# A hybrid decoder layer: level 3's differences between two halves of the masked copies, and a GpSimd product in two halves

## The reference

```
def gla_chunked(q, k, v, log_a):
    def step(state, inp):
        qc, kc, vc, ac = inp
        bc = jnp.cumsum(ac, axis=1)
        diff = bc[:, :, None] - bc[:, None, :]
        decay = jnp.exp(jnp.where(tri[None, :, :, None, None], diff, -jnp.inf))
        attn = jnp.einsum('bthd,bshd,btshd->bhts', qc, kc, decay)
        o = (jnp.einsum('bhts,bshv->bthv', attn, vc)
             + jnp.einsum('bthd,bhdv->bthv', qc * jnp.exp(bc), state))
        ...
        return new_state, o
...
    out_c = rms_norm(gla_chunked(qc, kc, vc, log_a), gla_out_gain).reshape(bsz, s, C_VWIDTH)
    mixed = jnp.concatenate([..., out_c.astype(h.dtype) * jax.nn.silu(cz)], axis=-1)
    return x + jnp.einsum('bse,ed->bsd', mixed, w_out)
```

## Time and profile before

| | us |
|---|---|
| median of three runs | 2102.72 |
| lowest and highest of them | 2099.99, 2103.46 |
| the profiled execution | 2099.63 |
| its span, first to last instruction | 2097.9 |
| TensorE busy in the span | 2038.0 (97%) |
| VectorE, ScalarE, GpSimd busy | 1023.9, 858.8, 390.9 |
| gated heads, four times (about 237 to 585) | 87 each |
| TensorE busy in them | 86.0, 86.3, 86.3, 86.3 |

### The profile page before, as it was taken

How to read it: one execution, slowest core, us unless ns; L and a number is a source line. 1 busy time by engine, 2 the same in 40 slices (tenths; PEclk the granted TensorE clock), 3 DMA queues, 4 the chain that set the end, 5 groups by cost and what they waited for, 6 DMA issues and landing times.

```text
span 2097.9 us, 28610 instructions
## 1 busy us (share of the span) xinstructions
PE 2038.0 (97%) x10084; PEld 1707.5 (81%) x10084; DVE 1023.9 (49%) x1615; ACT 858.8 (41%) x1434; POOL 390.9 (19%) x330
## 2 busy tenths in 40 slices
PE   6999999999999999999999999999999988999999
PEld 5778888888878888888888888888888867788887
DVE  6611356455545555465555555564555565512122
ACT  7311344434444444454444444454444454311110
POOL 0000344252422222121222212121222200000000
PEclk9999999999999999999999999999999999999999
DMA  6322333333232222222222222223222363423134
GB/s 227 77 73 67 104 78 105 108 90 107 70 96 76 75 80 67 85 75 85 65 70 85 75 86 86 80 83 99 62 90 85 120 220 113 128 86 131 48 128 150
DMA packets 192457, 201.10 MB, mean 96 GB/s; under 512 B 15992, under 2 KB 141992, under 8 KB 191232
## 3 DMA queue, kind: packets, MB, share of 16 engines
q1 hardware_dynamic: 175664, 169.70, 27.7%
q10 hardware_dynamic: 16720, 30.45, 3.9%
HBM read 151.33 MB, written 48.78 MB: 95 GB/s over the span
## 4 chain that ended last, share of the span: by engine, by line
PE 83%; DVE 8%; ACT 3%; issue 3%; DMA 2%; POOL 1%; SPq 0%; DVEq 0%; ACTq 0%; POOLq 0%
PE acc L1904 18%; PE acc L1906 17%; PE acc L1905 17%; PE pv L2122 4%; PE turned L2107 4%; PE scores L2099 2%; PE scores L2096 2%; DVE w_lo L1406 2%; PE scores L2212 1%; PE turned L2212 1%; PE acc L2212 1%; PE scores L2214 1%; PE turned L2214 1%; PE acc L2214 1%; PE scores L2213 1%
## 5 line engine op out<-in xcount | busy, mean ns | idle before, releaser
L1904 PE MATMUL acc<-act_hi,w_hi 128*128 128x512 f32 x1856 | 741.5, 400 | 6.5 <-DVE w_lo L1422 2.4
L1906 PE MATMUL acc<-act_hi,w_lo 128*128 128x512 f32 x1856 | 725.2, 391 | 0.0
L1905 PE MATMUL acc<-act_lo,w_hi 128*128 128x512 f32 x1856 | 724.0, 390 | 0.0
L1904 PEld LDWEIGHTS acc<-act_hi,w_hi 128*128 128x128 f32 x1856 | 349.0, 188 | 76.3 <-DVE w_lo L1406 5.8
L1906 PEld LDWEIGHTS acc<-act_hi,w_lo 128*128 128x128 f32 x1856 | 348.3, 188 | 75.9
L1905 PEld LDWEIGHTS acc<-act_lo,w_hi 128*128 128x128 f32 x1856 | 349.2, 188 | 65.2
L1406 DVE TENSOR_TENSOR w_lo<-w_raw,w_hi 128x512 fp32r<-128x512 f32 x223 | 203.0, 910 | 357.7 <-ACT w_hi L971 357.4
L1270 ACT ACTIVATE prob<-prob,neg_max 128x128 f32<-128x128 f32 (+7 forms) x160 | 124.0, 775 | 237.2 <-DVE neg_max L1714 237.2
L1730 DVE TENSOR_TENSOR pt_lo<-turned,pt_hi 128x1024 fp32r<-128x1024 f32 (+1 forms) x120 | 114.9, 958 | 168.8 <-ACT pt_hi L1278 168.5
L971 ACT ACTIVATE w_hi<-w_raw 128x512 fp32r<-128x512 f32 x223 | 139.1, 624 | 134.8 <-PE acc L1906 110.7
L1278 ACT ACTIVATE pt_hi<-turned 128x1024 fp32r<-128x1024 f32 (+1 forms) x120 | 97.5, 812 | 232.4 <-PE turned L2107 232.1
(11 more groups left out here) (315 smaller groups left out, 2876.5 us busy)
## 6 DMA issues: line engine op xcount, KB each, us to landing
w_raw<-in_w_in_dram SPq DMA_DIRECT2D x240, 256.0 KB, 2.9
proj_scratch<-stage ACTq DMA_DIRECT2D x116, 256.0 KB, 2.1
w_raw<-in_w_out_dram SPq DMA_DIRECT2D x71, 256.0 KB, 3.0
raw<-proj_scratch SPq DMA_DIRECT2D x20, 512.0 KB, 3.3
act_lo<-mixed_scratch SPq DMA_DIRECT2D x7, 1024.0 KB, 6.6
res<-in_x_dram SPq DMA_DIRECT2D x24, 256.0 KB, 5.5
out_dram<-res SPq DMA_DIRECT2D x24, 256.0 KB, 2.9
extra_raw<-in_w_out_dram SPq DMA_DIRECT2D x23, 256.0 KB, 3.3
```

The costliest lines, as they stand in the source:

```text
L1904: pe.matmul(acc, hi, xh, start=first, stop=False)
L1905: pe.matmul(acc, hi, xl, start=False, stop=False)
L1906: mm = pe.matmul(acc, lo, xh, start=False, stop=end)
```

## The change

Two edits, both in the gated heads.

1. The two differences of level 3 (`MIDWAY = 3`) leave slot 9 of VectorE. They are issued in slot 8, in `put_first`, behind the two copies of the first half of the weights and ahead of those of the second. Their code moves into a function, `level_diff`, which the other levels use where they were. Waits and operands stay as they are.
2. GpSimd's product of z and its sigmoid becomes two instructions of 96x1024, each of which raises `gla_silu`. VectorE's waits count two for a head: the gate of the next head waits for both, the final product for one half at a time.

```diff
--- before.py
+++ after.py
@@ -80,6 +80,7 @@
 G_BACK_V = 11
 G_LEVEL = [6 + l for l in range(LEVELS)]
 PUTS = 4 + LEVELS - 1
+MIDWAY = 3
 KEY_PARTS = 2 * (LEVELS - 1)
 LEVELS_READY = 4 + 4 * LEVELS
 
@@ -900,7 +901,8 @@
                     pool.tensor_tensor(places[:, :, ::-1] if e == 1 else places, keys, decays, ALU.mult).then_inc(gla_ke, 1)
 
                 pool.wait_ge(gla_sigmoid, c + 1)
-                pool.tensor_tensor(g_z[:, :, :], g_z[:, :, :], g_t[:, :, :], ALU.mult).then_inc(gla_silu, 1)
+                for h in range(2):
+                    pool.tensor_tensor(g_z[:, h, :], g_z[:, h, :], g_t[:, h, :], ALU.mult).then_inc(gla_silu, 1)
 
             gla_head(0)
             with pool.Fori(1, C_HEADS) as c:
@@ -1537,7 +1539,7 @@
                 if slot == G_GATE:
 
                     dve.wait_ge(gla_bias_in, 16 * (c + 1))
-                    dve.wait_ge(gla_silu, c)
+                    dve.wait_ge(gla_silu, 2 * c)
                     dve.wait_ge(gla_gate, c + 1)
                     dve.tensor_scalar(g_t[:, 0, :], scores[0:C_DK, :], gate_bias[:], None, ALU.add).then_inc(gla_sum, 1)
                 if slot == G_CLEAR:
@@ -1554,16 +1556,8 @@
                         dve.tensor_tensor_scan(out=g_b[:, at], data0=g_t[:, 0, at], data1=g_t[:, 0, at],
                                                    initial=0.0, op0=ALU.add, op1=ALU.bypass).then_inc(gla_scan, 1)
                 for l in range(LEVELS):
-                    if slot == G_LEVEL[l]:
-                        b, n = 1 << l, LEVELS * c + l
-                        if l == 0:
-                            dve.wait_ge(gla_scan, NT * (c + 1))
-                        bv, ev = blocks(g_b[:], b), blocks(g_t[:, l % 2, :], b)
-                        edge = bv[:, :, 0, b - 1:b].broadcast_to([C_DK, SEQ // (2 * b), b])
-
-                        dve.wait_ge(gla_ql, n - 1 if l >= 2 else LEVELS * c)
-                        dve.tensor_tensor(ev[:, :, 1, :], bv[:, :, 1, :], edge, ALU.subtract).then_inc(gla_diff, 1)
-                        dve.tensor_tensor(ev[:, :, 0, :], edge, bv[:, :, 0, :], ALU.subtract).then_inc(gla_diff, 1)
+                    if slot == G_LEVEL[l] and l != MIDWAY:
+                        level_diff(c, l)
                 if slot == G_LEVEL[0] + 2:
                     put_first(c)
                 for l in range(1, LEVELS - 1):
@@ -1602,12 +1596,23 @@
                     dve.tensor_tensor(o_rows, o_rows, o_rstd[:].unsqueeze(2).broadcast_to([P, NT, C_DV]), ALU.mult)\
                         .then_inc(gla_norm, 1)
                 if slot == G_FINAL:
-                    dve.wait_ge(gla_silu, c + 1)
                     for h in range(2):
+                        dve.wait_ge(gla_silu, 2 * c + h + 1)
                         dve.wait_ge(gla_ot, 2 * c + h + 1)
                         dve.scalar_tensor_tensor(out=g_z[:, h, :], in0=(scores, turned)[h][0:C_DK, :],
                                                      scalar=out_gain[:, h:h + 1], in1=g_z[:, h, :], op0=ALU.mult,
                                                      op1=ALU.mult).then_inc(gla_out, 1)
+
+            def level_diff(c, l):
+                b, n = 1 << l, LEVELS * c + l
+                if l == 0:
+                    dve.wait_ge(gla_scan, NT * (c + 1))
+                bv, ev = blocks(g_b[:], b), blocks(g_t[:, l % 2, :], b)
+                edge = bv[:, :, 0, b - 1:b].broadcast_to([C_DK, SEQ // (2 * b), b])
+
+                dve.wait_ge(gla_ql, n - 1 if l >= 2 else LEVELS * c)
+                dve.tensor_tensor(ev[:, :, 1, :], bv[:, :, 1, :], edge, ALU.subtract).then_inc(gla_diff, 1)
+                dve.tensor_tensor(ev[:, :, 0, :], edge, bv[:, :, 0, :], ALU.subtract).then_inc(gla_diff, 1)
 
             def put(dst, mask, data):
                 dve.reg_add(levels_put, levels_put, 1)
@@ -1619,6 +1624,7 @@
                 for half in range(2):
                     to = weights_t[:, half * HALF:(half + 1) * HALF].rearrange("p (b u q) -> p b u q", b=2, u=2)
                     if half > 0:
+                        level_diff(c, MIDWAY)
                         dve.wait_ge(gla_put, levels_put)
                     put(to, ident_both[:, :, :].unsqueeze(1).broadcast_to([P, 2, 2, P]), pieces[half][:, :, :, 0:P])
                     dve.wait_ge(gla_put, levels_put)
```

## The result

| | median, us | of |
|---|---|---|
| before | 2101.53 (2099.84 to 2103.46) | 10 runs |
| changed | 2108.68 (2105.47 to 2114.17) | 10 runs |
| ratio, with its 95% interval | 1.0037 (1.0025 to 1.0049) | |

The forecast was 2106.1 with 2100.8 to 2108.3. The kernel did get slower, by 7.15 us where 3.4 was forecast, and ends 0.4 us above the range. The forecast stood on a median of three runs, 2102.7; the ten runs give 2101.5, so the time misses by 2.6 us and the change by 3.8. The ten runs of the changed kernel also lie further apart than those of before: 8.7 us against 3.6. The profiled execution took 2106.12 us.

What follows compares the result with a forecast made beforehand. TensorE, busy 97% of the span, was taken as the bound, so only its waits counted. Moving the differences (+4.0 us) and halving the z product (-0.6) gave +3.4 on 2102.7: 2106.1 us, range 2100.8 to 2108.3.

Steps and rivals of the forecast that it cites:

- the rules of the replay: VectorE and GpSimd instructions exclude each other in arrival order; the blocked one starts 0.13 us before the blocker's recorded end.
- Part 1: Moving level 3's differences ahead: level 3's wait goes, but the turn of v starts about 1.0 us later per head; +4.0 us.
- K4: GpSimd's two halves of `k_level` for level 4; in head 1 the first was to start at 355.94, ahead of `w_lo`.
- Q4: GpSimd's `q_tile` product of level 4, 1.27 us, forecast to stand ahead of VectorE's second difference of level 5.
- D5b: VectorE's second difference of level 5, forecast to end at 360.04 in head 1 instead of 358.88.
- S: ScalarE's reversed copy of v, right behind level 5's exponential; forecast to end at 362.08 in head 1 instead of 360.92.
- Part 2: The z product in halves on GpSimd: 0.33 us free in heads 0 and 1, taken back in 2 and 3; -0.6 us.
- The sum: Over the four gated heads: +4.0 - 0.6 = +3.4 us, added to the three-run median 2102.7 for 2106.1 us.
- The spread: The forecast's own uncertainty, some 1.5 us: 0.2 us a head on the walk, and the spread of medians.
- The rivals: No effect, some 2101.5 us (chance 0.20); slower by much, 2111 (0.13); both edits pay in full, 2096.7 (0.03).
- slower by much: GpSimd's level-2 `q_tile` product goes ahead of VectorE's second level-3 difference; turn of v 2.25 us late; +8.4, 2111; chance 0.13.
- the signs named for "right": Turn of v waits about 1.4 us for ScalarE's copy in all heads; level 3 waits for nothing; `w_lo` takes about 2.4.

Runs made afterwards that it cites:

- mid_only: The changed kernel with the z product left as one instruction, so only level 3's differences move; 2110.55 us, ratio 1.0036 to before.
- s_twice: The kernel before with ScalarE's reversed copy of v made twice, so that TensorE waits for it; 2104.87 us, ratio 1.0019.
- even_first: The changed kernel with TensorE turning the even blocks of v first and waiting for the reversed copy only ahead of the odd ones; 2101.79 us.
- s_thrice: The kernel before with ScalarE's reversed copy of v made three times, for a longer TensorE wait; 2112.68 us, ratio 1.0068.
- q4_halves: The changed kernel with GpSimd's q_tile product of level 4 in two halves; 2102.72 us, ratio 1.0009 to before.
- filled: The changed kernel with 16 matmuls, their results overwritten by the same values, filling TensorE's wait before the turn of v; 2104.27 us.

## Why the prediction was wrong, point by point

- *What bounds the kernel, and the rules of the replay*: right. The rows of VectorE and GpSimd in head 1 are within 0.05 us of the walk, ScalarE's within 0.07, the turn of v within 0.03; only level 4 started 0.12 sooner than walked, since the 0.1 of restart did not come.
- *Part 1, +4.0*: measured +4.2. The wait for level 3 went, K4 came ahead of `w_lo`, Q4 ahead of D5b, and the turn of v waited for S in all four heads. A little was mis-sized: head 0's wait at level 4 grew by 0.43.
- *Part 2, -0.6*: measured -0.62, free in heads 0 and 1 and taken back in 2 and 3 by the normalisation.
- **The sum** is the step that failed. It took a wait of 1.4 us at its own length. In the profiled execution the granted clock went from its upper to its lower level behind that wait in two of four heads, and each time cost about 1.7 us, +3.4 together. The sum had no term for the clock and gave no reason for leaving it out. In the gated heads of the kernel before the clock was 1.00 and no wait of TensorE was longer than 0.7, so those heads said nothing on a wait twice as long. The rest of that trace did, and it points the other way: waits as long as this one, at other places, had no fall behind them. The longest of these under 2 us, and the clock from there on:

```profile
610.23 0.30 PE L2096 MATMUL scores<-k_hi,q_st 128*128 128x128 f32 x1 [1.88 <-issue]
```

```profile
610.00:613.00 3.00, 2.77 (x14) 2.42 (x15) 1.91 (x9) 1.84 (x5) 0.12 (x1) 1.00 0.65 228
```

The falls in that trace stand beside waits of 2.7 to 3.7 us, at the start and near the end of the span. So the missing term could have been seen to be open, but not its size: nothing at the least, and, priced afterwards by the runs, four falls of 1.65, 6.6 us and 2112.7, for a wait that falls once in each head (head 1 of mid_only lost 3.2).
- *The spread*: 1.5 us was too small, in all likelihood for the same reason. The changed kernel's runs spread over 8.7 us; the four slowest have a mean clock of 0.989 to 0.992, the six others 0.994 to 0.996. Where the clock fell in the runs that were not profiled isn't known.
- *The rivals*: none of them came. The one for "slower by much" had another place (D3b behind Q2): D3b went ahead, `w_lo` kept its deadline.
- *What would show it*: all the signs named for "right" came, and they could not tell 2106 from 2109; the clock was not among them.
- *Luck*: the direction and the terms of the sum were worked out, not guessed. But the starting median of three runs was 1.2 us above that of ten, and without that the forecast, 2104.9, would have been 3.8 short and not 2.6.

What stays open: what decides whether the clock falls in a head. The falls in profiled executions: in none of eight heads behind waits of 0.7 to 0.8 for S (s_twice, even_first), in two of four and four of four behind 1.3 to 1.4 (changed kernel, mid_only), in one of four behind 1.8 to 1.9 (s_thrice), and none behind the 1.3 at level 4 (q4_halves). In the changed kernel and in mid_only another wait, of 0.2 to 0.7 for level 4, ends some 2.5 us before the one for S does; in s_thrice and s_twice there is none so near. By itself that first wait is harmless (filled). Whether the two together bring the fall more often than one long wait is not shown: no run has a wait of 1.3 to 1.4 for S without one for level 4.

## What to carry over

Where an edit puts a new wait on a TensorE that never idles, price the wait and its clock apart, and give the second a bound even if the trace of before shows no fall; filling the wait with matmuls whose results don't matter is a quick test of which one you pay. Before moving an instruction ahead, walk through what both engines on a shared access have queued at that point: freed time in front of one of them can turn the order over further on, here two levels later. And look at what stands behind the delayed instruction on its own engine: the loss came from a copy that needed nothing of level 5 and merely stood behind it, and moving that copy turned the change into a gain.

## What the runs showed of the hardware

- The granted clock of TensorE fell in six of eight heads behind waits of 1.3 to 1.4 us out of nearly full activity: 0.60 and 0.68 over the 3 us at the turn in the changed kernel, with matmuls of 512 columns stepping by 0.42 instead of 0.23 and the turn's by 0.16 instead of 0.08. With 16 matmuls in the wait it stayed at 1.00. Waits as long elsewhere had no fall (1.88 at 610.23 of the kernel before, 1.28 at 274.11 of q4_halves).
- In these rows VectorE's differences and `w_lo`, each with two operands in SBUF, and GpSimd's products exclude each other one instruction at a time, in order of arrival, and the blocked one starts 0.12 to 0.13 us before the recorded end of the other. Splitting an instruction does not shorten the queue: the other engine's next one goes in between, and the second half waits for it. That pays where the one that goes in between is the urgent one: D5b with Q4 in halves (1.77, then 1.22), and `w_lo` with the z product in halves (4.68, then 2.47). With Q3 in halves it only moved the delay from D4a (1.34, then 0.79) to D4b (0.68, then 1.21).
